# Second mixture of a two-layer encoder: item rows come from memory in slot order, the products with w1 and w3 are made in column halves

## The reference, cut to what matters

```
def hier_moe(x2d, w_group, b_group, w_expert, b_expert, w1, w3, w2):
    g_prob = softmax(x2d @ w_group + b_group);      g_w, g_idx = top_k(g_prob, 1)
    e_prob = softmax(logits of the 4 experts of that group);  e_w, e_idx = top_k(e_prob, 2)
    combine[t, expert] = g_w * e_w / sum(e_w)       # two experts for each token
    for each expert e:
        h = silu(x2d @ w1[e]) * (x2d @ w3[e])       # 1024 -> 512
        out += combine[:, e] * (h @ w2[e])          # 512 -> 1024
h = layernorm(ALPHA * h + out)                      # both layers
```

## Time and profile before

| | |
|---|---|
| median of 3 runs | 797.28 us (791.65 to 798.72) |
| profiled execution | 795.07 us |
| its span, first to last instruction | 793.3 us |
| mean granted TensorE clock | 0.956 |
| PE busy | 703.1 us (89%) |
| second mixture, from its first hidden product to its last output | about 614.7 to 773 us of the span |

### The profile page before, as it was taken

How to read it: one execution, slowest core, us unless ns; L and a number is a source line. 1 busy time by engine, 2 the same in 40 slices (tenths; PEclk the granted TensorE clock), 3 DMA queues, 4 the chain that set the end, 5 groups by cost and what they waited for, 6 DMA issues and landing times.

```text
span 793.3 us, 19122 instructions
## 1 busy us (share of the span) xinstructions
PE 703.1 (89%) x7595; PEld 442.6 (56%) x7596; DVE 306.0 (39%) x928; ACT 218.6 (28%) x569; POOL 30.6 (4%) x46
## 2 busy tenths in 40 slices
PE   5999889878989989986879999977987999998985
PEld 4887558644545545543348547755854455554541
DVE  0799831382212222211244205873148122222226
ACT  1541350243212212211141013656023222222221
POOL 0000000110000000000200001110020000000010
PEclk9999999988999999998789999999997999999998
DMA  9999134204799699999799000030006995935924
GB/s 292 363 393 371 36 133 157 109 1 145 289 385 401 225 389 374 353 345 352 252 388 386 4 0 1 1 133 1 1 1 231 398 384 173 403 137 200 406 89 155
DMA packets 87080, 175.64 MB, mean 221 GB/s; under 512 B 7784, under 2 KB 21969, under 8 KB 87041
## 3 DMA queue, kind: packets, MB, share of 16 engines
q1 hardware_dynamic: 72912, 157.36, 54.1%
q10 hardware_dynamic: 11601, 8.20, 3.4%
q0 software_dynamic: 2528, 9.57, 3.2%
HBM read 163.06 MB, written 12.06 MB: 221 GB/s over the span
## 4 chain that ended last, share of the span: by engine, by line
PE 65%; DMA 14%; DVE 8%; ACT 5%; issue 4%; ACTq 2%; POOL 2%; SPq 0%; DVEq 0%; POOLq 0%
PE ps L735 16%; DMA ring<-in_moe_w 12%; PE ps L756 8%; PE ps L529 7%; PE ps L653 4%; PE ps L625 4%; PE ps L636 4%; PE ps L850 3%; PE ps L869 3%; PE ps L707 2%; PE ps L718 2%; PE ps L562 1%; PE ps L547 1%; POOL xT L481 1%; DVE work L1489 1%
## 5 line engine op out<-in xcount | busy, mean ns | idle before, releaser
L735 PE MATMUL ps<-ring,work 128*32 128x256 f32 x2816 | 171.1, 397 | 25.0 <-issue 16.5
L735 PEld LDWEIGHTS ps<-ring,work 128*32 128x32 f32 x2816 | 98.2, 114 | 91.0 <-issue 42.5
L959 ACT ACTIVATE work<-ps 128x256 f32<-128x256 f32 (+5 forms) x166 | 57.9, 364 | 238.7 <-PE ps L756 102.6
L1489 DVE TENSOR_TENSOR work<-work,ps 64x256 f32<-64x256 f32 x44 | 18.7, 424 | 217.1 <-ACT work L1070 217.1
L756 PE MATMUL ps<-ring,work 128*32 128x256 f32 x1408 | 90.1, 384 | 1.8 <-DMA ring<-in_moe_w 1.8
L707 PE MATMUL ps<-tok,work 128*32 128x256 f32 (+1 forms) x928 | 64.6, 385 | 2.2 <-DVE work L1472 2.2
L1250 DVE SCALAR_TENSOR_TENSOR work<-work,wdw 128x272 f32<-128x272 f32 x150 | 65.1, 494 | 1.0
L529 PE MATMUL ps<-xT,ring 128*128 128x272 f32 x256 | 60.6, 400 | 0.3 <-DVE xT L1227 0.3
L756 PEld LDWEIGHTS ps<-ring,work 128*32 128x32 f32 x1408 | 38.8, 109 | 37.8 <-DVE work L1491 13.1
L529 PEld LDWEIGHTS ps<-xT,ring 128*128 128x128 f32 x256 | 49.5, 194 | 10.8 <-DVE xT L1227 0.4
L1070 ACT ACTIVATE work<-ps 64x256 f32<-64x256 f32 x44 | 16.5, 375 | 112.8 <-PE ps L735 112.8
(11 more groups left out here) (249 smaller groups left out, 749.7 us busy)
## 6 DMA issues: line engine op xcount, KB each, us to landing
ring<-in_moe_w SPq DMA_DIRECT2D x120, 1024.0 KB, 12.0
ring<-in_conv_w_pw SPq DMA_DIRECT2D x12, 1024.0 KB, 11.9
ybuf<-work ACTq DMA_DIRECT2D x44, 128.0 KB
ybuf<-const POOLq DMA_DIRECT2D x2, 2560.0 KB, 9.4
ring<-in_kv_w_k SPq DMA_DIRECT2D x4, 1024.0 KB, 9.2
ring<-in_kv_w_v SPq DMA_DIRECT2D x4, 1024.0 KB, 10.8
ring<-in_attn_w_q SPq DMA_DIRECT2D x4, 1024.0 KB, 11.3
ring<-in_attn_w_o SPq DMA_DIRECT2D x4, 1024.0 KB, 10.8
```

Of the source, the lines that this page charges most:

```text
L735: last = pe.matmul(ps[SLOTS * q:SLOTS * (q + 1), 0, 0:256], xTg[:, k, :], w[:, k, (q % 2) * 256:(q % 2 + 1) * 256], start=(k == 0), stop=( ...
L959: return act.activation(dst, src, ACT.Copy)
```

## The change

Layer 0 keeps its items, but its ACT and the start of the program see two more DMA semaphore counts: a new DRAM buffer `xsort` (1152 rows of 4 KB) is filled with constants by POOL beside the fill of `ybuf`, before the first mixture.

In layer 1:

- POOL writes every token's row to its two slots of `xsort` with four indirect DMAs (`sort_rows`), as soon as DVE has the slots.
- DVE makes one selection for 96 slots (`pick3`) instead of one of 32 for each item, PE selects the first three items' rows at once (`gather_ahead`, 24 matmuls), ACT moves them.
- From the fourth item on ACT loads an item's rows from `xsort`, two items ahead of their use, into two buffers `rows_next`. The loads sit in ACT's queue before each item's output. DVE's and PE's per-item selection is gone.
- The hidden product is made in two halves of 128 columns of each quarter, in two PSUM banks (0 and 5): 64 matmuls of 128 columns instead of 32 of 256. Silu, gate, transpose and move come for each half; the first half's silu and gate can run under the second half's matmuls. The output product's parts 0 and 2 come before 1 and 3, with the second half's transpose between part 0 and part 2.
- The three item loops of PE carry a hint for the branch back.

The diff, cut to its core:

```diff
+        xsort = nc.dram_tensor("xsort", (SORTED * SLOTS, D), F32, kind="Internal").ap()
...
+            pool.dma_start(xsort.rearrange("(a p) d -> p a d", p=P),
+                           const[:, 0:D].unsqueeze(1).broadcast_to([P, SORTED * SLOTS // P, D])).then_inc(sem("y_filled"), 16)
+            def sort_rows():
+                pool.wait_ge(sem("y_filled"), 32)
+                pool.wait_ge(sem("sort_ready"), 1)
+                pool.wait_ge(sem("tok_ready"), 10)
+                for j in range(TILES[1]):
+                    for c in range(2):
+                        pool.indirect_dma_start(
+                            out=xsort, out_offset=bass.IndirectOffsetOnAxis(ap=sort_i[:, c * 2 + j:c * 2 + j + 1], axis=0),
+                            in_=tok[:, j, :], in_offset=None,
+                        ).then_inc(sem("xsort_ready"), 16)
...
+            def sorted_item(g, b, it):
+                def hidden(part):
+                    for k in range(NC_):
+                        if k % 4 == 0 and part == 0:
+                            for m in range(2):
+                                pe.wait_ge(*arrived(b + m, k // 4, it))
+                        for q in range(QUARTERS):
+                            at = (q % 2) * 256 + part * P
+                            last = pe.matmul(ps[SLOTS * q:SLOTS * (q + 1), HIDDEN_BANK[part], 0:P], xTg[:, k, :],
+                                             w[q // 2][:, k, at:at + P], start=(k == 0), stop=(k == NC_ - 1),
+                                             skip_group_check=True)
+                    return last
...
+                pe.wait_ge(sem("xT_ready1"), g + 1)
+                hidden(0).then_inc(sem("h_begun1"), 1)
+                hidden(1).then_inc(sem("h_ready1"), 1)
+                turn_hidden(0)
+                pe.wait_ge(sem("xg_here"), g + 1)
+                for m in range(2):
+                    last = pe.transpose(ps[:, 3, m * P:(m + 1) * P], xg[:, m * P:(m + 1) * P], ident)
+                last.then_inc(sem("xg_turned1"), 1)
+                pe.wait_ge(sem("hT_ready1"), g * 2 + 1)
+                pe.wait_ge(*arrived(b + 2, 0, it))
+                output(0, True, False)
+                turn_hidden(1)
+                pe.wait_ge(*arrived(b + 2, 1, it))
+                output(2, False, False)
+                pe.wait_ge(sem("hT_ready1"), g * 2 + 2)
+                output(1, False, False)
+                output(3, False, True).then_inc(sem("y_ready1"), 1)
...
+                def item(g, buf, turn):          # ACT
+                    act.wait_ge(sem("h_begun1"), g + 1)
+                    act.activation(hs[64:128, 0:P], ps[0:64, HIDDEN_BANK[0], 0:P], ACT.Silu).then_inc(sem("silu_ready1"), 1)
+                    act.wait_ge(sem(f"xg_loaded{buf}"), turn * 16 + 16)
+                    act.wait_ge(sem("xg_turned1"), g + 1)
+                    move(xg, rows_next[buf]).then_inc(sem("xg_here"), 1)
+                    act.wait_ge(sem("h_ready1"), g + 2)
+                    act.activation(hs[64:128, P:2 * P], ps[0:64, HIDDEN_BANK[1], 0:P], ACT.Silu).then_inc(sem("silu_ready1"), 1)
+                    act.wait_ge(sem("xsort_ready"), 16 * 2 * TILES[1])
+                    act.wait_ge(sem("xg_here"), g + 1)
+                    act.dma_start(rows_next[buf],
+                                  xsort[bass.ds((g + PICKED) * SLOTS, SLOTS), :].rearrange("s (q c) -> q s c", q=QUARTERS)).then_inc(sem(f"xg_loaded{buf}"), 16)
...
+                with dve.Fori(0, n) as g:
+                    gate(g, 0)
+                    move_hidden(g, 0)
+                    gate(g, 1)
+                    move_gathered(1, g + 1, True)
+                    move_hidden(g, 1)
```

More of the change, by code:

```diff
@@ L484, in _ @@
                 scale(l)
+                if l == 1:
+                    sort_rows()
                 pool.wait_ge(sem("tab_ready"), l + 1)
@@ L758, in item, with turn_hidden, output @@
                 last.then_inc(sem(f"y_ready{l}"), 1)
+            def sorted_item(g, b, it):
+                w = [brick(b + m).rearrange("p (k n) -> p k n", k=NC_) for m in range(2)]
+                w2 = brick(b + 2).rearrange("p (k n) -> p k n", k=4)
+                def hidden(part):
[9 more added lines that the diff above has]
+                    return last
+                def turn_hidden(part):
+                    pe.wait_ge(sem("hs_ready1"), g * 2 + (part + 1))
+                    pe.sem_inc(sem("turn_begun"), 1)
+                    pe.transpose(ps[:, 4, part * 64:(part + 1) * 64], hs[64:128, part * P:(part + 1) * P],
+                                 ident[64:128, 64:128]).then_inc(sem("h_turned1"), 1)
+                def output(k, first, final):
+                    for q in range(QUARTERS):
+                        last = pe.matmul(ps[SLOTS * q:SLOTS * (q + 1), 1, 0:256], hT[:, k, :], w2[:, k, q * 256:(q + 1) * 256],
+                                         start=first, stop=final, skip_group_check=True)
+                    return last
+                pe.wait_ge(sem("xT_ready1"), g + 1)
[15 more added lines that the diff above has]
+                output(3, False, True).then_inc(sem("y_ready1"), 1)
@@ L760, in mixture, with gather_ahead @@
+            def gather_ahead(i):
+                for j in range(TILES[1]):
+                    for q in range(QUARTERS):
+                        last = pe.matmul(ps[SLOTS * q:SLOTS * (q + 1), (2, 6, 7)[i], 0:256], pick3[:, j, i * SLOTS:(i + 1) * SLOTS],
+                                         tok[:, j, q * 256:(q + 1) * 256], start=(j == 0), stop=(j == TILES[1] - 1),
+                                         skip_group_check=True)
+                last.then_inc(sem("xg_ready1"), 1)
             def mixture(l):
@@ L766, in mixture @@
                 pe.wait_ge(sem("tab_ready"), l + 1)
-                gather(l, 0, True, range(TILES[l]))
-                turn_gathered(l, 0, True)
+                if l == 0:
+                    gather(l, 0, True, range(TILES[l]))
+                    turn_gathered(l, 0, True)
+                else:
+                    pe.wait_ge(sem("pick_ready1"), 1)
+                    gather_ahead(0)
+                    gather_ahead(1)
+                    turn_gathered(l, 0, True)
+                    gather_ahead(2)
                 pe.wait_ge(sem("late_pick_ready"), l + 1)
@@ L777, in expert @@
                     with pe.If(hi - lo):
-                        with pe.Fori(lo, hi) as g:
-                            item(l, g, b, it)
+                        if l == 0:
+                            with pe.Fori(lo, hi) as g:
+                                item(l, g, b, it)
+                        else:
+                            with nc.Fori(lo, hi, engines=bass.OrderedEngineSet([pe.engine]), hint_back_edge=True) as g:
+                                sorted_item(g, b, it)
                 with pe.Fori(0, live_groups) as it:
```

104 lines of the change are left out of this document (78 added, 26 removed).

## The result

The changed kernel takes 813.79 us (median, 812.79 to 815.61) against 796.02 us of the kernel before in the same sessions: a ratio of 1.0256, 95% interval 1.0215 to 1.0297, slower. The ratios in this document are the recorded estimates with their intervals; the quotient of two medians can differ from them by up to 0.3%, as here (1.0223). The forecast was 793, the range 785 to 805.

The account below looks back on a forecast made before the run. PE's item chain was taken to bound the second mixture, the weight stream its last stretch: -9.7 for items, -1.3 after them, +5.3 start writes, +1.5 clock, together -4.2 us from 797.28, forecast 793, range 785 to 805.

Parts of the forecast that it names:

- The item: Second mixture, PE's chain: an item takes 3.5 us hidden product plus 2.9 to the next, 6.4 us, 0.77 less.
- The upper bound by weight loads: Hidden product in halves: at 131 ns for each four weight loads it would take 4.2 us.
- Weight loads show: Rival: 108 ns streams no longer hide PE's weight loads, hidden product 4.2 us, total 802.6 us; chance 0.17.
- ACT: ACT's work per item is under 4.5 us of 6.4, so it doesn't bound; row loads have 12 us to land.
- The last sentence of the prediction: Forecast altogether wrong if ACT's row loads landed after 12 us and PE waited for the rows; no chance given.
- Branches: Rival: longer PE loop body makes two expert changes cost 2.15 us each, +4.3, total 797.4 us; chance 0.1.
- The start: Before the first item: sort_rows writes delay the first expert's weights 5.3 us, and PE's lower clock adds 1.5.
- The start is free: Rival: sort_rows writes go beside the weights and the clock recovers as before, total 786 us; chance 0.17.
- The last stretch: From fifteenth hidden product to twentieth item's output: last two experts' weights end last, 42.9 us against 44.2, gain 1.3.
- plus 2.0 for the row loads of six items: Last stretch: six row loads of 131 KB at 388 GB/s add 2.0 us to the weight stream.

Follow-up runs that it names:

- run 8: Changed kernel without the branch hint, row loads from the fourth item on issued by POOL on its own queue: 792.92 us, ratio 1.0011 to the kernel before.
- Run 4: Kernel before plus the xsort fill and writes, and ACT row loads per item that nobody reads: 813.51 us, ratio 1.0234.
- run 1: Changed kernel without ACT's row loads from xsort, hint and xsort writes kept: 797.15 us, ratio 1.0052 to the kernel before.
- run 6: Changed kernel without the branch hint and without the row loads: 787.08 us, ratio 0.9932 to the kernel before.
- run 5: Changed kernel without the branch hint, row loads kept in ACT's queue: 813.75 us, ratio 1.0273 to the kernel before.
- run 7: Kernel before with only the branch hint added on the second mixture's three item loops: 802.45 us, ratio 1.0141.
- run 3: Kernel before plus the xsort fill and the four scattered writes of sort_rows, results unread: 797.99 us, ratio 1.0047.
- Run 9: Kernel before plus xsort writes and unread row loads, each landing as 32 rows of 4 KB in 32 partitions: 799.28 us, ratio 1.0073.
- run 10: Changed kernel without hint, five items selected on PE, xsort writes held back, sixteen items' rows loaded at once by POOL: 792.87 us, ratio 1.0006 to before.
- run 12: Changed kernel without hint, xsort writes held back, six items selected on PE, POOL's row loads spread out: 788.92 us, ratio 0.9958 to the kernel before.
- run 2: Changed kernel, hint kept, all row loads including the second and third item's issued by POOL on its queue: 811.85 us, ratio 1.0209 to the kernel before.

## Why the prediction was wrong

**The item: right.** 6.34 us in after and 6.30 in run 8 against 6.4 forecast, the hidden product 3.49 against 3.50. The upper bound by weight loads (4.2) and the rival *Weight loads show* fell. What the prediction quoted from the Trainium skill, 81 ns for each matmul of 128 columns ("TensorE: Matmul & The Clock Gate", section "Back-to-back issue gap"), is no price for four tiles side by side: 128 records in 3.49 us are 27 ns each, or 109 ns for each tile's own stream.

**The step that failed** is the paragraph *ACT*: "The load has two items (12 us) to land", with "so it doesn't bound". I costed ACT by what it executes and the load by its bytes. The store already took its time behind the weights, and I asked only whether ACT's instructions fit into the item, not whether its DMA queue does. Run 4 shows what the second transfer for each item does, 1.0186 times the writes' 1.0047, without any other part of the change; run 1 shows it gone. The load takes 17 us where 12 were allowed for, and, what I had not seen at all, the stores in the same queue take 14 to 18 us from their issue to the move that waits for them. The last sentence of the prediction named this case and put no price or chance on it; it should have been a rival, the first one. Between runs 6 and 5, both without the hint, it is worth 19.5 us of B.

The Trainium skill, page "DMA: Bandwidth & Descriptors", section "Queues, rings and completion order", says that each DMA engine takes its queues in turn, a packet from each, and works through one ring in its order. The trace fits, though it shows no single turn: a transfer of 128 KB of ACT's can be used 14 to 18 us after its issue while 1 MB transfers of SP's land in 15.2. The Trainium skill, same page, section "Issuing engines are not separate DMA queues", says that another issuing engine saves little but the time of issuing. For B the runs show more than that: POOL's queue in place of ACT's took 22.4 us out of it (104.3 to 81.9, both without the hint). For C they agree, 51.4 and 49.9 (runs 5 and 8).

**The rival Branches** (0.1) had a real core, and I had argued it away with "between the experts inside a group no gap stands in the chain", which is true of code without the hint. It had forecast one stop at each of the two changes of expert before the fifteenth item, 4.3 us together, and run 1 has exactly these two, in the eighth and ninth item. The hint, which the prediction didn't price, makes them, and they cost 9.7 us of B where nothing covers them (run 1 against run 6), and 1.4% in the kernel before. In after, taking the hint out changes nothing (run 5), so the stops are no part of its 2.6%. The longer body, the rival's own reason, is not what it takes: run 7 has the old one. What the prediction quoted from the Trainium skill ("Runtime: NRT & Kernel Launch", section "Instruction fetch mechanics"), that a branch outside the part fetched ahead stalls, fits the place of the stops, behind a loop that is left. The packet of the instruction queue doesn't confirm it, since before has one in the same stretch without a stop; and of a hint the section says nothing.

**The start** is a size that was nearly right: 5.3 + 1.5 forecast, 5.8 measured, 5.2 of it by the writes alone (run 3). How much of that is the lower clock, the 1.5 of the forecast, no run tells apart. The rival *The start is free* fell.

**The last stretch.** The forecast's 42.9 contains 2.0 for row loads. Without the loads it had 40.9, and C is 42.3 in two runs, 1.4 more. The term that was mis-sized is "plus 2.0 for the row loads of six items". It is 7.6 to 9.1 us (runs 8 and 5 against run 6): in run 8 five loads cost 1.5 us each, over four times the time of their bytes. Run 9 shows that this goes with the form in which it lands.

Sum by the runs: start +5.8; items -8.4 (run 6's B; -11.3 where nothing stops PE) instead of -10.0; the row loads +18.1 in B, for which the forecast had nothing, and +7.9 in C instead of +2.0; C without loads -1.9 instead of -3.3. That is +21.5 against a forecast of -4.2, a miss of 25.7: ACT's queue in B is 18.1 of it, the row loads in C 5.9.

**Open:** what in a row load makes it dear, the 128 pieces or the 128 partitions, and why the output stores of before, in pieces as small, leave the weights at 388 GB/s. Also what PE waits for in the two stops, why changes of expert stop it with the hint in the first group of turns and not in the second, and why short stops remain in the ninth item without the hint (runs 6, 10 and 12).

## What to carry to other kernels

Cost a DMA by the queue that it joins as well as by its issue and its bytes: how many transfers of this form the queue finishes for each turn of the loop while the big stream runs, and whose completions lie behind the new one. Look in the trace at the transfer that is already there, from its issue to the first wait that it ends, and ask what two of it would take. A part of a change that looks like a free extra, here a hint on a branch, gets a line in the sum and a run of its own.

## What the runs showed of the hardware

- With a hint for the branch back on its item loops PE stops for 2.1 to 3.6 us (up to 4.8 in run 2) at two points of this program, each in the first item after a turn's loop is left; in the kernel before the hint costs 1.4% (run 7).
- A row load that is scattered over 128 partitions in pieces of 1 KB takes what all DMA engines move from 400 down to about 250 to 340 GB/s while it runs (run 8); sixteen in a burst hold it at 241 to 282 GB/s for 30 us, with the engines busy throughout (run 10). The same 128 KB in 32 rows of 4 KB cost next to nothing (run 9).
- 128 records of 128 columns on four tiles side by side take as long as 64 of 256: 3.49 us in after and 3.45 to 3.50 in before.
